# Two fused transformer blocks on one core: attention orders, a Fourier transform by symmetry, and modulation sums in another place

## The reference

```python
h = layer_norm(x, ...)
for l in range(2):                                   # first block
    q, k, v, u = split(h @ w_in[l])                  # 512 columns each
    a = diff_attention(q, k, v, ...)                 # 8 heads, each the difference of two softmaxes
    f = fourier_mix(u, w_f[l], b_f[l])               # 4 groups of 128 channels:
        # real(fft over the tokens of fft over the channels of u) @ w_f[g] + b_f
    h = layer_norm(ALPHA * h + concat(a, f) @ w_o[l], ...)
    h = layer_norm(ALPHA * h + swiglu(h), ...)       # width 2816
mod = silu(c) @ w_ada + b_ada                        # 9 rows of 1024: shift, scale, gate x 3
h += 0.5 * gate0 * swiglu(modulate(rmsnorm(h), shift0, scale0))   # second block
h += gate1 * mixer(modulate(rmsnorm(h), shift1, scale1))          # convolution, attention
h += 0.5 * gate2 * swiglu(modulate(rmsnorm(h), shift2, scale2))
out = rmsnorm(h)
```

## Time and profile before

| | |
|---|---|
| Median of 3 runs | 1269.5 us (1265.62 to 1269.55) |
| The profiled execution, its own time | 1267.37 us |
| Its span, first to last instruction | 1265.7 us |
| Busy: TensorE, VectorE, ScalarE, GpSimd | 1187.1, 809.9, 558.6, 116.5 us |
| Mean granted clock of TensorE | 0.977 of 2.4 GHz |
| Attention stage, layer 0 (scores(0) to residual) | 56.4 to 128.3 us |
| FFN, layer 0 (first full chunk to residual) | 145.8 to 331.4 us |

### The profile page before, as it was taken

One profiled execution on the slowest core, in us unless ns is written; L12 is line 12 of the kernel. 1 busy time (PEld: TensorE's weight loads), 2 busy tenths in 40 slices (PEclk: granted clock), 3 DMA queues, 4 the chain that ended last, 5 costly groups with the idle time before them and its releaser, 6 DMA issues.

```text
span 1265.7 us, 20129 instructions
## 1 busy us (share of the span) xinstructions
PE 1187.1 (94%) x7988; PEld 1075.8 (85%) x7988; DVE 809.9 (64%) x1037; ACT 558.6 (44%) x645; POOL 116.5 (9%) x98
## 2 busy tenths in 40 slices
PE   5978899999997889999978999998999999999997
PEld 4856899999686679999968999996998997999996
DVE  6454957777665586777767577776468467545454
ACT  4554443343345543434324434343497435433332
POOL 3300520000160133000000000000000000000000
PEclk9999999999999899999988999998999999999999
DMA  9511376667171137677725577661533552645550
GB/s 370 211 67 67 136 280 262 265 265 286 67 265 38 65 135 280 236 278 293 272 99 200 191 273 290 265 245 65 213 105 107 199 190 100 233 170 195 182 182 34
DMA packets 34850, 242.93 MB, mean 192 GB/s; under 512 B 3792, under 2 KB 5216, under 8 KB 8048
## 3 DMA queue, kind: packets, MB, share of 16 engines
q1 hardware_dynamic: 27792, 196.29, 41.9%
q0 software_dynamic: 5520, 45.17, 9.7%
q10 hardware_dynamic: 1488, 0.76, 0.2%
HBM read 241.16 MB, written 1.05 MB: 191 GB/s over the span
## 4 chain that ended last, share of the span: by engine, by line
PE 82%; DVE 8%; ACT 5%; issue 2%; DMA 1%; POOL 0%; SPq 0%; DVEq 0%; ACTq 0%
PE bank L412 76%; DVE w_lo L1092 1%; ACT w_hi L784 1%; ACT work L898 1%; DVE x_lo L1165 1%; PE bank L523 1%; DVE small L1108 1%; DMA raw<-stream 1%; PE bank L529 1%; PE bank L585 1%; DVE h L1121 1%; PE bank L487 1%; PE bank L567 1%; PE bank L544 1%; DVE h L1141 1%
## 5 line engine op out<-in xcount | busy, mean ns | idle before, releaser
L1092 DVE TENSOR_TENSOR w_lo<-raw,w_hi 128x2048 fp32r<-128x2048 f32 x184 | 431.9, 2352 | 223.3 <-ACT w_hi L784 223.2
L412 PE MATMUL bank<-x_hi,w_hi 128*128 128x256 f32 x1824 | 520.8, 286 | 4.0 <-DVE x_lo L1165 1.7
L412 PE MATMUL bank<-x_lo,w_hi 128*128 128x256 f32 x1824 | 516.5, 283 | 0.0
L412 PE MATMUL bank<-x_hi,w_lo 128*128 128x256 f32 x1824 | 516.3, 283 | 0.0
L784 ACT ACTIVATE w_hi<-raw 128x2048 fp32r<-128x2048 f32 x184 | 351.1, 1908 | 176.8 <-PE bank L412 169.6
L412 PEld LDWEIGHTS bank<-x_hi,w_hi 128*128 128x128 f32 x1824 | 350.2, 192 | 11.0 <-issue 5.4
L412 PEld LDWEIGHTS bank<-x_lo,w_hi 128*128 128x128 f32 x1824 | 350.3, 192 | 2.3 <-issue 0.5
L412 PEld LDWEIGHTS bank<-x_hi,w_lo 128*128 128x128 f32 x1824 | 350.3, 192 | 0.0
L412 PE MATMUL bank<-w_hi,hid_hi 128*128 128x512 f32 x352 | 141.9, 403 | 0.0
L412 PE MATMUL bank<-w_lo,hid_hi 128*128 128x512 f32 x352 | 139.7, 397 | 0.0
L412 PE MATMUL bank<-w_hi,hid_lo 128*128 128x512 f32 x352 | 139.7, 397 | 0.0
(11 more groups left out here) (151 smaller groups left out, 1113.9 us busy)
## 6 DMA issues: line engine op xcount, KB each, us to landing
raw<-stream SPq DMA_DIRECT2D x184, 1024.0 KB, 4.8
work<-ada POOLq DMA_DIRECT2D x24, 1536.0 KB, 7.6
gain_rows<-rows POOLq DMA_DIRECT2D x11, 512.0 KB, 6.7
gate_rows<-rows POOLq DMA_DIRECT2D x3, 512.0 KB, 11.5
c<-consts SPq DMA_DIRECT2D x1, 1218.0 KB, 13.6
h<-x SPq DMA_DIRECT2D x4, 256.0 KB, 4.5
out<-z SPq DMA_DIRECT2D x4, 256.0 KB, 2.1
wf<-w_f ACTq DMA_DIRECT2D x2, 256.0 KB, 11.8
```

Of the source, the lines that this page charges most:

```text
L412: last = nc.tensor.matmul(out, stationary, moving, start=start and i == 0, stop=stop and i == 2, skip_group_check=True)
L1092: nc.vector.tensor_tensor(w_lo[j % SLOTS][:, :], raw[j % SLOTS][:, :], w_hi[j % SLOTS][:, :].bitcast(F32), ALU.subtract).then_inc(lo_ready, 1)
```

## The change

It has four parts.

- **Fourier.** The transform over tokens keeps 129 cosine and 127 sine columns (`COS` = 129) instead of 256 and 256, since cosine is even and sine odd in the frequency. `fourier_features` fills the other half of the output from the same columns read backwards, with four matmuls of 129, 127, 127 and 127 columns instead of two of 256; for the odd part the table is kept a second time with its sign turned (`keep_tables`, three copies). `P_s` halves, and so does the table in the constants. In layer 1 the table matmuls move from ahead of `transposes` to between the V and the U projections, as in layer 0.
- **Order.** In both layers the heads, Fourier pieces, splits of chunks 8 to 12 and output rows stand in another order on TensorE, ScalarE and VectorE.
- **Gates.** The gate part of `ada_acc` is split into fp32r parts, in `mix_hi` and `mix_lo`, which are free in the FFN: ScalarE copies it, after a wait for the last `ada_step`, ahead of the last step's SiLU; VectorE subtracts, ahead of the last product. `sum_gates` multiplies both with fp32r ones in four matmuls of 512 columns, at the place of `sum_ada`.
- **Shifts.** `sum_shifts`, the 16 one-column fp32 matmuls, follows the last down product and writes to bank 1; `keep_shifts` stands ahead of the next `input_split` on VectorE, and TensorE waits for it (`ada_kept`) before it uses the bank.

```diff
@@ -372,6 +377,7 @@
             nc.gpsimd.memset(neg_half, -0.5).then_inc(neg_half_ready, 1)
+            nc.gpsimd.memset(ones_r[:, :].bitcast(F32), 1.0).then_inc(ones_ready, 1)
             pool.dma_start(cp[:, :], common_params).then_inc(common_landed, 16)
...
@@ -513,21 +519,29 @@
                 if with_ada:
-                    sum_ada(f)
+                    sum_gates(f)
                 ffn_down(t, j + 3 * FT - 1, FT * f + (FT - 1), last_step=True)
-
-            def sum_ada(f):
-
-                pe.wait_ge(ada_step, KT * ADA_STEPS * f + KT * ADA_STEPS)
+                if with_ada:
+                    sum_shifts(f)
+
+            def sum_gates(f):
+
+                pe.wait_ge(ones_ready, 1)
+                pe.wait_ge(acc_ready, f + 1)
+                pe.wait_ge(silu_done, FT * f + FT)
+                for c, bank in ((0, B[3]), (1, B[0])):
+                    for i, part in enumerate((mix_hi, mix_lo)):
+                        last = nc.tensor.matmul(bank[:, :], ones_r[:, :],
+                                                part[:, 2 * c:2 * c + 2, :].rearrange("p k n -> p (k n)"),
+                                                start=i == 0, stop=i == 1)
+                last.then_inc(gates_reduced, 1)
+
+            def sum_shifts(f):
+
                 for q in range(SHIFT_SCALE):
-                    last = nc.tensor.matmul(B[2][:, q:q + 1], ada_acc[:, q * P:(q + 1) * P], ones[:, 0:1],
+                    last = nc.tensor.matmul(B[1][:, q:q + 1], ada_acc[:, q * P:(q + 1) * P], ones[:, 0:1],
                                             start=True, stop=True, skip_group_check=True)
                 last.then_inc(shifts_reduced, 1)
-                pe.wait_ge(silu_done, FT * f + FT)
-                for c, bank in ((0, B[3]), (1, B[0])):
-                    at = SHIFT_SCALE * P + c * HALF
-                    last = nc.tensor.matmul(bank[:, :], ones, ada_acc[:, at:at + HALF], start=True, stop=True)
-                last.then_inc(gates_reduced, 1)
...
@@ -582,16 +596,21 @@
                     for m in range(2):
-                        last = nc.tensor.matmul(B[1][:, :], u_s[:, m, g * P:(g + 1) * P], dft_s[:, m, :],
+                        last = nc.tensor.matmul(B[1][:, 0:S], u_s[:, m, g * P:(g + 1) * P], dft_s[:, m, :],
                                                 start=m == 0, stop=m == 1)
...
                     pe.wait_ge(P_ready, 4 * l + (g + 1))
-                    for c in range(2):
-                        last = nc.tensor.matmul(B[1][:, 0:S], tables[:, c, g * P:(g + 1) * P],
-                                                P_s[:, c * S:(c + 1) * S], start=c == 0, stop=c == 1)
-                    last.then_inc(y_done, 1)
+                    cos, sin, minus_sin = (tables[:, c, g * P:(g + 1) * P] for c in range(3))
+                    nc.tensor.matmul(B[1][:, 0:COS], cos, P_s[:, 0:COS], start=True, stop=False,
+                                     skip_group_check=True)
+                    nc.tensor.matmul(B[1][:, COS:S], cos, P_s[:, COS - 2:0:-1], start=False, stop=False,
+                                     skip_group_check=True)
+                    nc.tensor.matmul(B[1][:, 1:COS - 1], sin, P_s[:, COS:S], start=False, stop=True,
+                                     skip_group_check=True)
+                    nc.tensor.matmul(B[1][:, COS:S], minus_sin, P_s[:, S - 1:COS - 1:-1], start=False, stop=True,
+                                     skip_group_check=True).then_inc(y_done, 1)
...
@@ -612,16 +631,12 @@
-                if l > 0:
-                    pe.wait_ge(gates_kept, 2 * l)
-                    fourier_tables(B[0:2])
                 transposes(2 * l)
                 if l > 0:
-                    pe.wait_ge(tables_kept, 2 * l + 2)
+                    pe.wait_ge(ada_kept, l)
                 for c in range(2):
                     token_projection(t, V0 + c, B[0:2], c, input_tile(2 * l))
-                if l == 0:
-                    fourier_tables(B[6:8])
+                fourier_tables()
                 for c in range(2):
...
@@ -630,56 +645,58 @@
                 pe.wait_ge(proj_evac, 8 * l + 6)
-                pe.wait_ge(tables_kept, 2 * l + 2)
+                pe.wait_ge(tables_kept, 3 * l + 3)
                 scores(0)
-                projection(t, Q1, B[0], x_hi, x_lo, ks=range(2, 7))
+                projection(t, Q1, B[0], x_hi, x_lo, ks=range(2, 6))
                 scores(1)
                 transpose_a(0)
-                projection(t, Q1, B[0], x_hi, x_lo, ks=range(7, 8))
+                projection(t, Q1, B[0], x_hi, x_lo, ks=range(6, 8))
+                values(0)
                 fourier_tokens(0)
-                values(0)
                 transpose_a(1)
...
                 values(1)
+                transpose_a(2)
+                projection(t, K1, B[0], x_hi, x_lo, ks=range(2, 4))
+                values(2)
                 fourier_features(0)
-                projection(t, K1, B[0], x_hi, x_lo, ks=range(2, 4))
-                transpose_a(2)
+                transpose_a(3)
                 projection(t, K1, B[0], x_hi, x_lo, ks=range(4, 6))
-                values(2)
-                transpose_a(3)
+                values(3)
+                projection(t, K1, B[0], x_hi, x_lo, ks=range(6, 8))
                 fourier_tokens(1)
-                projection(t, K1, B[0], x_hi, x_lo, ks=range(6, 8))
-                values(3)
-                fourier_features(1)
                 pe.wait_ge(proj_evac, 8 * l + 8)
                 scores(2)
-                fourier_tokens(2)
-                fourier_features(2)
+                fourier_features(1)
+                transpose_o(0)
                 scores(3)
                 transpose_a(4)
-                transpose_o(0)
-                fourier_tokens(3)
+                fourier_tokens(2)
                 values(4)
                 transpose_a(5)
-                fourier_features(3)
+                fourier_features(2)
                 values(5)
+                transpose_a(6)
+                fourier_tokens(3)
                 pe.wait_ge(biased, 16 * l + 16)
                 mixed_row(0, 4)
-                transpose_a(6)
-                mixed_row(0, 5)
                 values(6)
                 transpose_a(7)
+                fourier_features(3)
+                values(7)
+                mixed_row(0, 5)
                 mixed_row(1, 6)
-                values(7)
                 mixed_row(1, 7)
-                to_residual(t, O0 + 2, mix_hi, mix_lo, (0, 1), False, False, mixed_tile)
+                mixed_row(2, 0)
                 transpose_o(1)
+                mixed_row(2, 1)
                 to_residual(t, O0 + 3, mix_hi, mix_lo, (2, 3), False, True, mixed_tile)
...
             transposes(5)
+            pe.wait_ge(ada_kept, 2)
             ffn(FFN1_T, 0, 2, 5, True)
...
@@ -719,6 +736,7 @@
+            pe.wait_ge(ada_kept, 3)
             for c in range(2):
...
@@ -835,6 +853,10 @@
                 t = t + (FT - 3)
+                if with_ada:
+                    act.wait_ge(ada_step, KT * ADA_STEPS * (f + 1))
+                    nc.scalar.activation(mix_hi[:, 0:4, :].rearrange("p k n -> p (k n)"),
+                                         ada_acc[:, SHIFT_SCALE * P:], ACT.Copy).then_inc(acc_hi_ready, 1)
                 after_gate(t, j + 5, FT * f + (FT - 1))
...
@@ -885,10 +907,12 @@
-                def keep_tables(banks):
-                    for c in range(2):
+                def keep_tables():
+                    for c, sign in ((0, 1.0), (1, 1.0), (1, -1.0)):
                         act.wait_ge(tables_done, 2 * l + c + 1)
-                        nc.scalar.activation(tables[:, c, :], banks[c][:, :], ACT.Copy).then_inc(tables_kept, 1)
+                        at = 2 if sign < 0 else c
+                        nc.scalar.activation(tables[:, at, :], B[6 + c][:, :], ACT.Copy, scale=sign)\
+                            .then_inc(tables_kept, 1)
...
@@ -950,49 +972,49 @@
                 keep_aT(0)
+                exps(2)
                 keep_query(Q1)
                 keep_P(0)
-                exps(2)
                 keep_aT(1)
+                exps(3)
+                keep_aT(2)
+                split(t, 8)
                 mix_fourier(0)
-                exps(3)
-                split(t, 8)
-                keep_aT(2)
                 keep_aT(3)
-                keep_P(1)
-                keep_key(K1)
-                mix_fourier(1)
                 head_squares(0)
                 split(t, 9)
+                keep_key(K1)
+                keep_P(1)
                 exps(4)
+                mix_fourier(1)
+                exps(5)
+                mix_attention(0)
+                keep_aT(4)
                 keep_P(2)
-                exps(5)
+                exps(6)
+                keep_aT(5)
                 mix_fourier(2)
-                exps(6)
-                keep_aT(4)
-                mix_attention(0)
+                exps(7)
+                keep_aT(6)
```

(75 more changed lines are left out.)

1 line of the change is left out of this document (removed).

## The result

Over four runs each, the changed kernel takes 1237.35 us (1236.16 to 1238.25) and the kernel before 1268.15 us (1265.62 to 1269.55): a ratio of 0.9745 [0.9718, 0.9772]. The forecast was 1240. The profiled execution took 1238.25 us, with a span of 1236.6 us.

A forecast was written before the change was run, and what follows sets the result against it. TensorE, busy 1187 of 1265.7 us, was taken as the bound, with chains of waits at FFN ends and in attention. Savings of 7.4 (FFNs) and 21.0 (attention), 28.4 us, gave 1239.0 from 1267.4, stated as 1240, range 1232 to 1252.

The forecast's parts named there:

- step 1: Ends of three FFNs, TensorE alone: gate matmuls take 0.94 us, residual 6.0 us sooner in the first, 7.5 in others.
- Step 2: FFN ends: ScalarE's copy waits for the last accumulation ahead of the SiLU, so only 2.4, 4.0 and 3.9 us are saved.
- The rival that the wait costs nothing: FFN ends: ScalarE's wait is free, so 16 us are gained instead of 7.4, giving 1231; chance 0.08.
- Step 3: Behind the FFN ends: layer 1's start loses 0.9 us to slower transposes and 1.7 to tables; the third FFN loses 0.3.
- The clock at V0: Rival: lower clock outlasts the V chunk's matmuls after slow transposes, 3.1 us in layer 1 and mixer, 1246; chance 0.05.
- Step 4: Attention in two layers: new order and halved token columns save 10.5 us a layer, 21.0 in all; backward reads cost nothing.
- the walk: Attention's new lists followed on paper with the old durations: residual at 117.1 instead of 128.34, 11.2 us a layer.
- clock 1.00 throughout: Sign expected in the profile after: TensorE's granted clock stays at 1.00 through the attention stages.
- a clock of 0.5 in it: Sign that the prediction is wrong: a granted clock of 0.5 within attention.
- the second rival: Clock falls in attention over short fp32 steps between 80 and 94 us, 3 us a layer, 1246; chance 0.07.
- Backward reads: Token transform's reversed column reads in attention: counted as nothing; rival that they make the kernel slower, 1275, chance 0.03.
- The start: Before attention: constants have 256 KB less, counted as nothing, at most 0.6 us sooner.

The follow-up runs named there:

- the second experiment: Layer 1's table matmuls moved between the two V chunks, against the changed kernel: 1236.18 us, 0.9756 of the kernel before.
- the first experiment: ScalarE's copy of the gate part moved behind the SiLU and the rounding of chunk j+8, against the changed kernel: 1227.28 us, 0.9687 of the kernel before.
- the FFN part: Changed kernel with old attention order and old Fourier transform, keeping gates, shifts and layer 1's table place: 1261.91 us, 0.9946 of the kernel before.
- the last two: Changed kernel with copy behind SiLU, tables between V chunks, combine(3) before chunk 8's split: 1220.6 us; plus K1's copy, head 4's biases before chunk 9's split: 1221.35.

## Why the prediction was right

- **What bounds, and step 1.** The four fp32r matmuls take 0.93 us as said (0.94), at full clock. What TensorE alone could win was 6.0 and 7.5; with the copy moved the runs gave 6.6, 8.0 and 7.5.
- **Step 2**, which decides most: 13.44 us from the last accumulation to the residual for 13.41; -2.5 for -2.4 and -4.0 for -3.9. The second FFN gave 4.7 for 4.0; of that 0.6 are faster transposes at its start (1.78 us for ten instead of 2.41), which I had not looked for. The rival that the wait costs nothing had 16 us for the FFNs where steps 2 and 3 measured 8.2; moving the copy wins 10 to 11.
- **Step 3**: +2.6 for +2.6. The transposes cost 0.9 up to V1 for 0.9, the tables 1.7 for 1.7. The 0.3 at the mixer did not come there, but nearly the same is lost later on (+0.4 over R5 to the end).
- **The clock at V0.** I took it as hidden. In this profile there was nothing to hide: the lower level ended before V0's first matmul (granted clock 0.90 in 330:331, V0 from 330.33), so its absence from the time is no proof of the room beside it. That room was 1.0 us and not 1.6, as V0 started 3.9 us after the transposes and not 3.4. In the second experiment the lower level did reach V0, for 1.6 us, and took 0.7 of that room. The rule named with that rival (the Trainium skill, TensorE: Matmul & The Clock Gate, Part 4: transposes do not count as PE activity as matmuls do) changed no term here. The runs do not settle it: behind the sums of the first experiment the clock stayed at 1.00 through ten transposes and beyond.
- **Step 4, attention**: 21.4 us for 21.0. In layer 1 the stations of the walk were met; in layer 0 they were up to scores(2), which came 1.9 us late. By kinds, with the 2.0 to 2.2 us of wait inside scores(3) counted as the walk counts them, layer 1 is as said: waits fell by 6.3 us for 6.0 (4.3, and 1.7 for the residual), the rest of busy time by 5.5 (59.49 to about 54.0) for 5.4 (3.2 of columns and 2.2 of clock). In layer 0 waits fell by 6.5 (12.45 to about 5.95), but the rest of busy time by only 3.1 (59.45 to about 56.35). The term that failed is the clock's: "clock 1.00 throughout" was false in both layers, "a clock of 0.5 in it" stood among the signs of being wrong, and layer 0 did not win the 2.2 us. That is the second rival in kind, which came true inside the forecast. That the sum is right within 0.4 us is luck: I had taken 10.5 a layer for a walk of 11.2 to 11.4, for small pieces that the walk leaves out, and this allowance of 1.8 us in all came near the 2.2 that the clock took back. Columns gave 2.8 a layer for 3.2.
- **Backward reads**: 0.22 to 0.28 us from one step to the next, either way. Step 4's "nothing" stands.
- **Which part gives what.** The order gives 8.6 us a layer with wide tokens (72.7, the average of the kernel before and the FFN part, to 64.1) and 9.7 with narrow ones (71.0 to 61.3); the columns give 1.7 in the old order (72.7 to 71.0) and 2.8 in the new one (64.1 to 61.3). The medians agree for the old order: 3.3 us for both layers (1261.91 to 1258.62). Whether order and columns help each other is not shown, as two stages of the same code differ by up to 3.1 us.
- **The start**: +0.4 for 0. The spans from the first instruction to scores(0) vary over 55.5 to 57.4 us among the profiles, so this is no cost of the change.

Open: why the clock falls at head 3's wait in four of eight stages and not in the others, with the same idle time ahead of it. The runs show that it does, not what decides it.

## What to carry to other kernels

A wait put on an engine's list is paid by all that stands behind it: the ScalarE copy cost 10 to 11 us in three places though its own result was in time, so place a copy of late data behind the work that is ready. Take an operation off an engine where that engine sets the end, and look at the order first: here it was worth 8.6 to 9.7 us a layer, the halved transform 1.7 to 2.8. Look for waits inside busy time too: a group of matmuls that takes three times what the same group takes elsewhere at the same clock holds a wait, here one for its banks. When the idle time before a station is named, follow what takes its place; the last such move here (head 4's biases) only exchanged one wait for another.

## What was not expected of the hardware

- The same list of attention instructions took 60.0 us in one layer and 62.8 in the other, with ScalarE and VectorE equally busy (37.5 and 37.7 us, 38.2 and 38.3); a repeat turned the two about. The old list took 71.9 three times and 75.0 once. The difference is in TensorE's busy time at a granted clock of 0.97 against 0.92, and 0.95 against 0.91. The kernel before, with more idle time, also spreads wider: 1263.3 to 1275.1 us in 15 runs on one chip, the changed one 1234.6 to 1238.5 in 4.
- The one-column sums keep TensorE busy, and yet the clock can fall under them: to about half near their end in the kernel before, and 2.4 us after their start in the changed one (0.69 in 323:324). In the first experiment they pass at 1.00, and the transposes right behind them take 1.17 us for ten, for 2.41 where the clock had fallen. That is no rule: in the three kernels with the copy moved (the first and the last two) the sums run straight into transposes at six places, and all 16 transposes take 1.95 us at three of them and 3.48 to 3.65 at the other three. No experiment told these apart.
